# Gated recurrence: the low weights of the fourth output chunk move from VectorE to GpSimd, with a semaphore of their own

## What is computed

```python
def rglru_mixer(h, w_in, conv_w, conv_b, w_a, b_a, w_i, b_i, lam, w_out):
    gate, u = jnp.split(h @ w_in, 2, axis=-1)
    u = causal_depthwise_conv(u, conv_w) + conv_b
    ...
    r = jax.nn.sigmoid(jnp.einsum("bsnc,ncd->bsnd", ub, w_a) + b_a).reshape(bsz, seq, LRU_WIDTH)
    i = jax.nn.sigmoid(jnp.einsum("bsnc,ncd->bsnd", ub, w_i) + b_i).reshape(bsz, seq, LRU_WIDTH)
    ...
    _, hs = lax.associative_scan(_lru_combine, (a, b), axis=1)
    y = jax.nn.gelu(gate) * hs.astype(h.dtype)
    return y @ w_out
```

## Time and profile before

| | |
|---|---|
| median of 3 runs | 2238.26 us (2237.91 to 2238.66) |
| the profiled execution | 2238.35 us, of which the span is 2236.6 us |
| busy share of the span | PE 94%, DVE 32%, ACT 29%, POOL 2% |
| granted clock of TensorE | 0.998 on average |
| end of the output products' first token tile, chunk 2 (TensorE idle after it) | 1.90 us idle at 1964.8 us |
| end of the junction on TensorE's first row of the second token tile | 1984.61 us |

### The profile page before, as it was taken

The page is one execution under the profiler, slowest core; times in us unless marked ns, Lnnn a source line. Parts: engine busy times, 40 slices in busy tenths (PEclk is TensorE's granted clock), DMA queues, the critical chain, the costliest instruction groups (busy, mean ns, idle before and its releaser), DMA issues.

```text
span 2236.6 us, 27188 instructions
## 1 busy us (share of the span) xinstructions
PE 2110.2 (94%) x12048; PEld 1295.8 (58%) x12048; DVE 725.7 (32%) x1041; ACT 642.5 (29%) x1024; POOL 42.7 (2%) x73
## 2 busy tenths in 40 slices
PE   9999999999899989999999899999999999999999
PEld 9987443333333333333333333337888998988997
DVE  8983110010010010010010010016665564876553
ACT  6664110010010010010010010005565444965442
POOL 3101000000000000000000000000000000000000
PEclk9999999999999999999999999999999999999999
DMA  8539999999999999999999999997444656544553
GB/s 239 175 96 383 416 402 430 430 425 430 429 425 430 430 425 430 429 425 429 429 425 430 429 422 429 430 425 238 141 170 155 203 188 197 175 157 151 198 189 113
DMA packets 153551, 725.21 MB, mean 324 GB/s; under 512 B 8662, under 2 KB 106378, under 8 KB 127962
## 3 DMA queue, kind: packets, MB, share of 16 engines
q1 hardware_dynamic: 152248, 721.47, 80.8%
q0 software_dynamic: 608, 1.36, 0.2%
q10 hardware_dynamic: 578, 0.64, 0.1%
HBM read 722.38 MB, written 1.07 MB: 323 GB/s over the span
## 4 chain that ended last, share of the span: by engine, by line
PE 57%; DMA 32%; DVE 7%; ACT 4%; issue 1%; SPq 0%; DVEq 0%; ACTq 0%
PE bank L1356 22%; PE bank L1232 17%; DMA weight_ring<-in_w_up_dram 12%; DMA weight_ring<-in_w_gate_dram 11%; DMA weight_ring<-in_w_down_dram 8%; PE bank L1191 5%; PE bank L1314 4%; PE bank L1385 2%; DVE weights_ring L2442 1%; PE bank L1162 1%; PE bank L1048 1%; DVE arena L2502 1%; ACT squares L2065 1%; PE bank L1289 1%; PE bank L1571 1%
## 5 line engine op out<-in xcount | busy, mean ns | idle before, releaser
L1232 PE MATMUL bank<-weight_ring,arena 128*64 128x506 f32 x3036 | 644.9, 563 | 37.3 <-DMA weight_ring<-in_w_gate_dram 19.0
L1232 PEld LDWEIGHTS bank<-weight_ring,arena 128*64 128x64 f32 x3036 | 213.0, 134 | 429.2 <-issue 388.4
L1314 PE MATMUL bank<-weight_ring,arena 128*64 128x512 f32 x1408 | 315.9, 599 | 66.8 <-DMA weight_ring<-in_w_down_dram 66.6
L2802 DVE SCALAR_TENSOR_TENSOR arena<-arena,bank 128x506 f32<-128x506 f32 (+1 forms) x48 | 28.0, 638 | 912.9 <-ACT arena L2035 912.9
L2834 DVE TENSOR_TENSOR weights_ring<-weight_ring,weights_ring 128x2048 fp32r<-128x2048 f32 x110 | 249.8, 2289 | 126.6 <-ACT weights_ring L2136 126.3
L1314 PEld LDWEIGHTS bank<-weight_ring,arena 128*64 128x64 f32 x1408 | 98.4, 138 | 273.4 <-issue 185.8
L1356 PE MATMUL bank<-input_high,weights_ring 128*128 128x256 f32 x1920 | 247.6, 280 | 0.8 <-issue 0.8
L1356 PEld LDWEIGHTS bank<-input_high,weights_ring 128*128 128x128 f32 x1920 | 234.2, 188 | 2.9 <-issue 2.5
L2136 ACT ACTIVATE weights_ring<-weight_ring 128x2048 fp32r<-128x2048 f32 x109 | 205.6, 1908 | 60.3 <-DMA weight_ring<-in_w_ffn_down_dram 40.9
L1191 PE MATMUL bank<-arena 128*128 128x256 f32 x512 | 142.9, 404 | 0.0
L1191 PEld LDWEIGHTS bank<-arena 128*128 128x128 f32 x512 | 87.3, 189 | 82.6 <-issue 75.6
(11 more groups left out here) (425 smaller groups left out, 1970.2 us busy)
## 6 DMA issues: line engine op xcount, KB each, us to landing
weight_ring<-in_w_down_dram SPq DMA_DIRECT2D x62, 2816.0 KB, 21.7
weight_ring<-in_w_up_dram SPq DMA_DIRECT2D x61, 2816.0 KB, 20.0
weight_ring<-in_w_gate_dram SPq DMA_DIRECT2D x60, 2816.0 KB, 19.1
weight_ring<-in_w_ffn_gu_dram SPq DMA_DIRECT2D x44, 1024.0 KB, 5.1
weight_ring<-in_w_ffn_down_dram SPq DMA_DIRECT2D x22, 1024.0 KB, 4.8
weight_ring<-in_w_in_dram SPq DMA_DIRECT2D x16, 1024.0 KB, 5.9
arena<-in_w_xkv_dram SPq DMA_DIRECT2D x8, 2048.0 KB, 23.4
weight_ring<-in_ab_w_in_dram SPq DMA_DIRECT2D x12, 1024.0 KB, 7.7
```

What stands on the lines that cost most here:

```text
L1232: last = pe.matmul(bank[first_bank + c][MPAD * half:MPAD * half + MPAD, 0:(hi - lo) * HF], xs3[:, s, :], rows[:, :, HF * half:HF * half + HF],
L1314: last = pe.matmul(bank[6][MPAD * half:MPAD * half + MPAD, :], hidT[:, at:at + MPAD], W[:, j * D + 512 * half:j * D + 512 * half + 512], s ...
L2802: dve.scalar_tensor_tensor(out=v, in0=v, scalar=1.0, in1=bank[c][:, 0:HF * (hi - lo)], op0=ALU.add, op1=ALU.mult)\
```

## The change

GpSimd gets one more instruction at the end of its list: it waits for the high part of the fourth output chunk (`c_out`, 3) and forms the low part, a subtraction of 128x2048, and signals on a new semaphore `pool_low`. TensorE waits for `pool_low` instead of `weights_low` where it takes that chunk. VectorE skips the chunk. So that the counts of `weights_low` stay positions in the sequence, VectorE waits for `pool_low` before the next chunk (`xq1`, 0) and raises `weights_low` by 2 there.

```diff
+        pool_chunk = c_index["c_out", 3]
...
             pool.tensor_copy(fox_pick, fpick).then_inc(S("fox_tables"), 1)
+            pool.wait_ge(S("weights_high"), NA + split_index[pool_chunk] + 1)
+            pool.tensor_tensor(low_slot(pool_chunk), raw_slot(pool_chunk), high_slot(pool_chunk), ALU.subtract).then_inc(S("pool_low"), 1)
...
                     pe.wait_ge(S("weights_high"), NA + n + 1)
-                    pe.wait_ge(S("weights_low"), NA + n + 1)
+                    if k == pool_chunk:
+                        pe.wait_ge(S("pool_low"), 1)
+                    else:
+                        pe.wait_ge(S("weights_low"), NA + n + 1)
...
                     k = split_chunks[n]
+                    splits[0] += 1
+                    if k == pool_chunk:
+                        continue
                     dve.wait_ge(S("weights_high"), NA + n + 1)
-                    dve.tensor_tensor(low_slot(k), raw_slot(k), high_slot(k), ALU.subtract).then_inc(S("weights_low"), 1)
-                    splits[0] += 1
+                    if split_chunks[n - 1] == pool_chunk:
+                        dve.wait_ge(S("pool_low"), 1)
+                    dve.tensor_tensor(low_slot(k), raw_slot(k), high_slot(k), ALU.subtract)\
+                       .then_inc(S("weights_low"), 2 if split_chunks[n - 1] == pool_chunk else 1)
```

## The result

The changed kernel takes 2243.04 us (median of 16 runs), the kernel before 2238.09 us beside it: ratio 1.0020, 95% interval 1.0014 to 1.0027. A second set of runs (the first experiment) gave 2243.05 against 2239.10, 1.0017 (1.0009 to 1.0026). The forecast was 2242.3, 4.0 us above before; measured were 4.95 and 3.95 us. Slower by about the 0.2% that can be told from no change.

What follows compares the result with a forecast made beforehand. TensorE, busy 94% of the span, was taken to bound the kernel. VectorE's delay of 4.27 us less 0.23 gained gave 4.04; 2238.26 + 4.04 = 2242.3 us, range 2241.0 to 2244.2.

Steps and rivals of the forecast that it cites:

- Part 1: Subtraction leaves VectorE: TensorE's 1.90 us wait goes, but only 0.23 us is gained at the second tile's transposes.
- Part 2: GpSimd's subtraction of 2048 columns takes 4.53 us (4.49 to 4.58), starting at 1957.23 when ScalarE's cast ends.
- the date of the start hardly matters: If VectorE's L3170 were issued before GpSimd's subtraction, L3163 behind it would be hit by the same amount.
- Part 3: GpSimd's subtraction shuts VectorE out for its whole length; VectorE's multiplication L3170 ends 4.27 us late.
- Part 4: VectorE and ScalarE pass the 4.27 us delay on without slack; the junction is 4.04 us late.
- (2,0): TensorE's product on chunk 2's low weights: starts at 1966.05 after a wait of 4.2 us, runs 2.8 us.
- The wait of 0.7 us at the first tile's transposes: TensorE reaches the first tile's transposes at 1978.65 and waits there about 0.7 us.
- (3,0): TensorE's product on the fourth output chunk: starts at 1968.85, 2.16 us later than before, covered by TensorE's slack.
- The rival with the clock: TensorE's clock halves for (2,0): 0.7 us more at the junction, 2243.0 us; chance 0.14 together with a longer GpSimd hold.
- The sum: Whole kernel: 4.04 us added to the median 2238.26 gives 2242.3 us, 0.18% slower.

Runs made afterwards that it cites:

- the first experiment: The changed kernel run once more, word for word, for an undisturbed trace, beside the kernel before: 2243.05 against 2239.10 us, ratio 1.0017.
- the kernel that does it alone: Changed kernel without GpSimd's subtraction; TensorE multiplies with the fourth output chunk's high weights in place of its low ones: 2238.95 against 2239.10 us, 1.0001.
- The memsets: Kernel before plus two GpSimd memsets of 128x2048 at the place of the change, VectorE keeping its subtraction: 2238.86 against 2239.10 us, 0.9998.
- the filled version: Changed kernel plus 14 small TensorE matmuls ahead of its wait for chunk 2's low weights: 2242.53 against 2238.85 us, 1.0016.

## Why the prediction was right

- **Part 1, 0.23 us.** Right in kind, 0.32 us by the kernel that does it alone; in the change the squares behind ScalarE's casts moved by +4.37 and +4.13, so 0.24 is the second one's small wait, and the other 0.09 comes up to B.
- **Part 2, the length.** 4.62 us against 4.53, just outside 4.49 to 4.58. The start, as ScalarE's cast ends, was right. No run had VectorE's instruction go first, so that the date of the start hardly matters stays untested.
- **Part 3, the exclusion.** Right: 4.37 us against 4.27, nearly all of the difference from part 2 (4.62 for 4.53). It fell on the instruction that was named, L3170. The memsets show the condition that the rows of before could not: GpSimd has to read.
- **Part 4, who pays.** +4.04 at B against +4.04 forecast. That the two agree to the last digit is luck: a hold 0.10 us too short and a gain 0.09 us too small cancel. TensorE waited 3.84 us, not 4.2: (2,0) starts where it should (8.80 us behind A, forecast 8.70), but TensorE came to the wait later: the last two matmuls of (1,0) start 4.33 us behind A (1962.76), where before they start 3.95 behind (1961.30). The wait of 0.7 us at the first tile's transposes is there at full clock (0.52 in the filled version) and was eaten by the lower clock in the change.
- **(3,0), wrong by 1.7 us.** It was forecast 2.16 us later than before. It starts at 1971.64 (the third matmul of a merged row), 13.21 us behind A against 9.34, +3.87: the clock. The rival with the clock had this at "0.7 us more" if it fell; it fell, and cost nothing at B. The step that failed in that rival is the size: 2.8 us of loss against some 2 us of slack. The fall lasted 3.4 us, of which half, 1.7 us, is lost, and the slack covered it.
- **The sum.** 4.04 by the trace at B and 3.75 at the end; 3.95 and 4.95 us by two pairs of medians, the larger one with a median of before 1.0 us below that of the second set.

One sentence ahead of the prediction is wrong: the matmuls of rounded operands have one record each (12 products are 12 records of 0.23 us, 2.8 us); two records each have the plain float32 ones, as the 14 that were read as x28.

## What to carry to other kernels

An engine with nothing to do is not free if it shares a way to memory with a busy one: ask what each of its instructions reads, and lay its length on the busiest instruction of the other. Read a wait past its end: TensorE's 1.90 us were worth 0.3, because ScalarE's casts held the next date anyway, and 0.9 once a subtraction on VectorE had moved. Three moves together (that subtraction, TensorE's high products first, one of the casts later) won 1.5 us in this stretch. Where medians differ by as little as their own spread, compare distances between two instructions of one trace.

## What the runs showed of the hardware

The granted clock of TensorE fell to 1.2 GHz for some 3.4 us after idle times of 3.84, 4.03, 1.84 and 1.79 us, and stayed at 2.4 GHz after 1.91, 1.90, 1.73, 1.73 and 1.71 us. One kernel gave both (1.84 and 1.71 us), so the kernel alone does not decide; nor does the length, since the clock stayed up after 1.90 and 1.91 and fell after 1.79. It cost 1.6 us where a chain hung on TensorE's next product and nothing where another engine held the next date. What decides it at idle times below 2 us stays open.

GpSimd's subtraction of 2048 columns took 4.62 us with VectorE waiting, a copy 1.90 and a memset 1.82; its 1024-column half 2.41.
